# Up-projection of a two-layer decoder trunk: high and low input parts in one 512-column product, the two bank halves added afterwards

## What is computed

```python
h = causal_depthwise_conv(x @ w_ffn_up[i], ffn_conv_w[i], ffn_conv_b[i])   # 2048 -> 2 * 5632, three taps in time
gate, up = jnp.split(h, 2, axis=-1)
ffn = (jax.nn.silu(gate) * up) @ w_ffn_down[i]                              # 5632 -> 2048
ple = (p[i] @ w_ple_proj[i]) * jax.nn.sigmoid(x @ w_ple_gate[i] + b_ple_gate[i])
x = layer_norm(DEEPNORM_ALPHA * x + ffn + ple, ln2_g[i], ln2_b[i])
```

## Time and profile before

| | |
|---|---|
| median of 3 runs | 2536.94 us (2536.22 to 2538.70) |
| span of the profiled execution | 2539.3 us (no other time of this execution is known) |
| TensorE busy in it | 2443.3 us, 96% |
| TensorE weight loads | 2191.4 us, 86% |
| VectorE busy | 1474.3 us, 58% |
| ScalarE busy | 1095.2 us, 43% |
| mean granted TensorE clock | 0.987 |
| layer 1, up-projection loop | 515 to 1022 us |
| layer 2, up-projection loop | 1773 to 2280 us |

### The profile page before, as it was taken

How to read it: one execution, slowest core, us unless ns; L and a number is a source line. 1 busy time by engine, 2 the same in 40 slices (tenths; PEclk the granted TensorE clock), 3 DMA queues, 4 the chain that set the end, 5 groups by cost and what they waited for, 6 DMA issues and landing times.

```text
span 2539.3 us, 38833 instructions
## 1 busy us (share of the span) xinstructions
PE 2443.3 (96%) x15144; PEld 2191.4 (86%) x15144; DVE 1474.3 (58%) x1397; ACT 1095.2 (43%) x1109; POOL 210.8 (8%) x121
## 2 busy tenths in 40 slices
PE   6899999999999999999988999999999999999997
PEld 6777887899999999888777778878999999998885
DVE  4566656475655566544555756564655566565446
ACT  3355435344444444444443554353444444443443
POOL 0144201000000000000011432010000000000000
PEclk9999999999999999999989999999999999999998
DMA  7444555565555555555544444655555555555552
GB/s 230 161 155 146 162 204 184 197 199 182 182 182 182 182 182 182 182 198 189 176 157 161 152 149 149 218 191 190 199 182 182 182 182 182 182 182 184 196 196 102
DMA packets 168228, 455.36 MB, mean 179 GB/s; under 512 B 7545, under 2 KB 11945, under 8 KB 148945
## 3 DMA queue, kind: packets, MB, share of 16 engines
q1 hardware_dynamic: 165536, 440.58, 51.2%
q0 software_dynamic: 2608, 13.69, 1.5%
HBM read 452.14 MB, written 2.10 MB: 179 GB/s over the span
## 4 chain that ended last, share of the span: by engine, by line
PE 85%; issue 7%; DVE 5%; ACT 2%; DMA 1%; POOL 0%; SPq 0%; DVEq 0%; POOLq 0%; ACTq 0%
PE ps L1081 83%; PE ps L1101 1%; ACT w_hi L522 1%; DMA xt<-in_x 0%; DVE w_lo L768 0%; PE ps L1234 0%; DVE xt L822 0%; DVE small L892 0%; DVE xt L818 0%; DVE scratch L895 0%; DMA vec<-in_ln_b 0%; PE ps L1178 0%; PE ps L1205 0%; DVE xT_lo L774 0%; DVE xt L794 0%
## 5 line engine op out<-in xcount | busy, mean ns | idle before, releaser
L768 DVE TENSOR_TENSOR w_lo<-raw,w_hi 128x2048 fp32r<-128x2048 f32 x416 | 969.0, 2330 | 1019.6 <-ACT w_hi L522 1016.7
L522 ACT CAST w_hi<-raw 128x2048 fp32r<-128x2048 f32 x416 | 793.2, 1907 | 1341.9 <-PE ps L1081 1341.9
L1081 PE MATMUL ps<-xT_hi,w_lo 128*128 128x256 f32 x2816 | 797.1, 283 | 1.5 <-DVE work L1025 1.5
L1081 PE MATMUL ps<-xT_lo,w_hi 128*128 128x256 f32 x2816 | 796.9, 283 | 0.0
L1081 PE MATMUL ps<-xT_hi,w_hi 128*128 128x256 f32 x2816 | 796.9, 283 | 0.0
L1081 PE MATMUL ps<-w_lo,xT_hi 128*128 128x512 f32 (+1 forms) x1920 | 753.7, 393 | 34.9 <-DVE w_lo L768 16.5
L1081 PE MATMUL ps<-w_hi,xT_lo 128*128 128x512 f32 (+1 forms) x1920 | 745.2, 388 | 0.0
L1081 PE MATMUL ps<-w_hi,xT_hi 128*128 128x512 f32 (+1 forms) x1920 | 744.9, 388 | 0.0
L1081 PEld LDWEIGHTS ps<-xT_hi,w_lo 128*128 128x128 f32 x2816 | 540.6, 192 | 2.3 <-issue 2.3
L1081 PEld LDWEIGHTS ps<-xT_hi,w_hi 128*128 128x128 f32 x2816 | 540.7, 192 | 0.0
L1081 PEld LDWEIGHTS ps<-xT_lo,w_hi 128*128 128x128 f32 x2816 | 540.7, 192 | 0.0
(11 more groups left out here) (141 smaller groups left out, 1010.1 us busy)
## 6 DMA issues: line engine op xcount, KB each, us to landing
raw<-in_w_ffn_up SPq DMA_DIRECT2D x176, 1024.0 KB, 5.0
raw<-in_w_ffn_down SPq DMA_DIRECT2D x88, 1024.0 KB, 4.8
raw<-in_w_in SPq DMA_DIRECT2D x84, 1024.0 KB, 5.0
raw<-in_w_out SPq DMA_DIRECT2D x32, 1024.0 KB, 5.4
raw<-in_w_ple_gate SPq DMA_DIRECT2D x32, 1024.0 KB, 4.8
vec<-in_ln_g POOLq DMA_DIRECT2D x4, 1024.0 KB, 6.4
vec<-in_ln_b POOLq DMA_DIRECT2D x4, 1024.0 KB, 6.1
raw<-in_w_ple_proj SPq DMA_DIRECT2D x4, 1024.0 KB, 4.8
```

Source lines behind the costliest of these rows:

```text
L522: nc.scalar.copy(w_hi[:, at % SPLIT_SLOTS, :], raw[:, at % RAW_SLOTS, :]).then_inc(hi_split, 1)
L768: tt(w_lo[:, at % SPLIT_SLOTS, :], raw[:, at % RAW_SLOTS, :], w_hi[:, at % SPLIT_SLOTS, :].bitcast(F32), ALU.subtract).then_inc(panels_spl ...
L1081: done = mm(bank, lhs, rhs, start=first and n == 0, stop=last and n == 2, skip_group_check=flip)
```

## The change

`x_hi` and `x_lo` become the two halves of one tile, so that 512 adjacent columns are [x_hi | x_lo] of an input chunk. For each pair (k, c) the two products with w_hi become one matmul of 512 columns into a whole bank, columns 0 to 255 for x_hi and 256 to 511 for x_lo; w_lo by x_hi, 256 columns, is added in the first half of the bank. A half now needs four banks: gate 0 to 3, up 4 to 7. In convolution step 0 ACT copies the second halves of the four banks to SBUF (two instructions of two banks), and DVE adds the first halves to them (two instructions); that sum, `summed`, is what frees the banks, by the new semaphores `gate_summed` and `up_summed`. The convolution reads the sum from SBUF and moves one step back: ACT's four instructions to step 1, DVE's eight to steps 1 and 2, sigmoid and final product to step 3, together with the taps. TensorE waits for the second and fourth `ple_sums` in place of the first and second, and starts the down-projection in the plain order.

```diff
-        xT_hi = sb("xT_hi", [P, KD, SEQ], F32R)
-        xT_lo = sb("xT_lo", [P, KD, SEQ], F32R)
+        xT = sb("xT", [P, KD, 2, SEQ], F32R)
+        xT_hi, xT_lo = xT[:, :, 0, :], xT[:, :, 1, :]
...
+        summed = scratch[:, 0:1024].rearrange("p (c t) -> p c t", t=SEQ)
+        x_lo_part = scratch[:, 1024:2048].rearrange("p (c t) -> p c t", t=SEQ)
...
                 def begin_conv(half, p, i):
-                    if p < 2:
+                    if p == 0:
                         act.wait_ge(panels_used, used(l, UP_AT + 4 * half + 4) + i * UP_BODY)
+                        for c in (0, 2):
+                            nc.scalar.copy(x_lo_part[:, c:c + 2, :],
+                                           ps[:, 4 * half + c:4 * half + c + 2, SEQ:]).then_inc(x_lo_copied, 1)
+                    elif p == 1:
                         act.wait_ge(conv_group_set, layered(l, TAPS, half + 1) + i * 2)
-                        for c in (2 * p, 2 * p + 1):
+                        act.wait_ge((gate_summed, up_summed)[half], layered(l, FF_GROUPS, 2) + i)
+                        stand_alone(act)
+                        for c in range(FF_GROUP):
...
                             last = nc.scalar.activation(
-                                dst, ps[:, 2 * half + p, (c % 2) * SEQ:(c % 2 + 1) * SEQ], ACT.Identity,
+                                dst, summed[:, c, :], ACT.Identity,
                                 bias=conv_group[:, 3, half, c:c + 1], scale=conv_group[:, 2, half, c:c + 1])
-                        last.then_inc(conv_begun, 1)
-                    elif p == 2 and half == 0:
+                            if c % 2:
+                                last.then_inc(conv_begun, 1)
+                    elif p == 3 and half == 0:
...
                 for j in range(4):
                     if j == 0:
                         begin_conv(1, 0, FF_GROUPS - 1)
+                    down_step(j + 1, 0)
+                    if j == 1:
                         begin_conv(1, 1, FF_GROUPS - 1)
-                    down_step(j + 1, 0)
...
-                def convolve(half, p, i):
+                def convolve(half, p, i, taps=True):
-                    if p < 2:
-                        dve.wait_ge(conv_begun, layered(l, 4 * FF_GROUPS, 2 * half + p + 1) + i * 4)
+                    if p == 0:
+                        for c in (0, 2):
+                            dve.wait_ge(x_lo_copied, layered(l, 4 * FF_GROUPS, 2 * half + c // 2 + 1) + i * 4)
+                            stand_alone(dve)
+                            link(tt(summed[:, c:c + 2, :], ps[:, 4 * half + c:4 * half + c + 2, 0:SEQ],
+                                    x_lo_part[:, c:c + 2, :], ALU.add))
+                        dve.sem_inc((gate_summed, up_summed)[half], 1)
+                    elif p < 3:
+                        dve.wait_ge(conv_begun, layered(l, 4 * FF_GROUPS, 2 * half + p) + i * 4)
                         for back in (1, 2):
-                            for c in (2 * p, 2 * p + 1):
-                                u = ps[:, 2 * half + p, (c % 2) * SEQ:(c % 2 + 1) * SEQ - back]
+                            for c in (2 * p - 2, 2 * p - 1):
...
-                        if p == 1:
-                            dve.sem_inc((gate_conv, up_taken)[half], 1)
-                    elif p == 2:
+                        if p == 2 and half == 0:
+                            dve.sem_inc(gate_conv, 1)
+                    else:
+                        if taps:
+                            set_taps(1 - half, i + half)
                         if half == 0:
                             dve.wait_ge(gate_sigmoid, layered(l, FF_GROUPS, 1) + i)
+                            stand_alone(dve)
                         link(tt(group, group, tmp[half], ALU.mult))
-                    else:
-                        set_taps(1 - half, i + half)
...
+            def columns_by_tokens(l, at, i, first_bank, first_chunk, first, last):
+
+                pe.wait_ge(panels_split, layered(l, PANELS, at + 1 + RAW_SLOTS) + i * UP_BODY)
+                s = at % SPLIT_SLOTS
+                for k in range(4):
+                    for c in range(FF_GROUP):
+                        w = slice(k * 512 + c * P, k * 512 + (c + 1) * P)
+                        x = xT[:, first_chunk + k, :, :].rearrange("p s t -> p (s t)")
+                        if first and k == 0:
+                            mm(ps[:, first_bank + c, :], w_hi[:, s, w], x, start=True, stop=False)
+                        done = mm(ps[:, first_bank + c, 0:SEQ], w_lo[:, s, w], xT_hi[:, first_chunk + k, :],
+                                  start=False, stop=False, skip_group_check=True)
+                        if not (first and k == 0):
+                            done = mm(ps[:, first_bank + c, :], w_hi[:, s, w], x, start=False, stop=last and k == 3)
+                done.then_inc(panels_used, 1)
...
-                        pe.wait_ge(ple_sums, layered(l, 4, half + 1))
-                        pe.wait_ge((gate_conv, up_taken)[half], layered(l, FF_GROUPS, 1) + i)
+                        pe.wait_ge(ple_sums, layered(l, 4, 2 * half + 2))
+                        pe.wait_ge((gate_summed, up_summed)[half], layered(l, FF_GROUPS, 1) + i)
+                        stand_alone(pe)
                         for j in range(4):
...
+                            columns_by_tokens(l, UP_AT + 4 * half + j, i, 4 * half, 4 * j, j == 0, j == 3)
...
-                order = [(1, n) for n in range(4)] + [(0, n) for n in range(4)]
-                waits = {(0, 0): (gate_conv, layered(l, FF_GROUPS, FF_GROUPS + 1)),
-                         (0, 2): (up_taken, layered(l, FF_GROUPS, FF_GROUPS + 1))}
+                waits = {(0, 0): (gate_summed, layered(l, FF_GROUPS, FF_GROUPS + 1)),
+                         (1, 0): (up_summed, layered(l, FF_GROUPS, FF_GROUPS + 1))}
```

More of the change, by code:

```diff
@@ L324, in build, with chunks @@
         pool_step = sem("pool_step")
+        def chunks(bank):
+            return ps[:, bank, :].rearrange("p (k t) -> p k t", t=SEQ)
         def rotate(tt, link, heads, table, m, rot_a, rot_b):
@@ L826, in _ @@
             dve.sem_inc(panels_split, RAW_SLOTS)
[L828 to L829 removed]
+            dve.sem_inc(gate_summed, 1)
+            dve.sem_inc(up_summed, 1)
             dve.sem_inc(left_normed, M)
@@ L1053, in _ @@
                         convolve(1, 0, FF_GROUPS - 1)
-                        convolve(1, 1, FF_GROUPS - 1)
                     down_step(j + 1, 0)
-                    if j == 1:
-                        convolve(1, 2, FF_GROUPS - 1)
+                    if j:
+                        convolve(1, j, FF_GROUPS - 1, taps=False)
                 stand_alone(dve)
@@ L1069, in _ @@
             mm = nc.tensor.matmul
+            def columns_by_tokens(l, at, i, first_bank, first_chunk, first, last):
[12 more added lines that the diff above has]
+                done.then_inc(panels_used, 1)
             def panel(l, at, i, step, products, show=False):
                 pe.wait_ge(panels_split, layered(l, PANELS, at + 1 + RAW_SLOTS) + i * step)
-                for at_product, (bank, hi, lo, x_hi, x_lo, first, last, flip, wait) in enumerate(products):
+                for at_product, (bank, hi, lo, x_hi, x_lo, first, last, wait) in enumerate(products):
                     if wait:
@@ L1079, in panel @@
                     for n, (x, w) in enumerate(pairs):
-                        lhs, rhs = (w, x) if flip else (x, w)
-                        done = mm(bank, lhs, rhs, start=first and n == 0, stop=last and n == 2,
-                                  skip_group_check=flip)
+                        done = mm(bank, x, w, start=first and n == 0, stop=last and n == 2)
                     if show and last and at_product < len(products) - 1:
@@ L1096, in tokens_by_columns @@
                         found.append((banks(m, n)[:, 0:hi - lo], w_hi[:, s, lo:hi], w_lo[:, s, lo:hi], xh[x], xl[x],
-                                      first and k == 0, last and k == k_chunks - 1, False, waits.get((m, n))))
+                                      first and k == 0, last and k == k_chunks - 1, waits.get((m, n))))
                 return found
@@ L1367, in down @@
+                def down(j, i, first=False, last=False, waits={}):
                     pe.wait_ge(g_split, layered(l, KFF, j + 1) + i * 4)
-                    wide(l, DOWN_AT + j, j, first, last, i=i, step=4, order=order, waits=waits, show=True)
-                down(0, 0, first=True, order=order, waits=waits)
+                    wide(l, DOWN_AT + j, j, first, last, i=i, step=4, waits=waits, show=True)
+                down(0, 0, first=True, waits=waits)
                 for j in range(1, 4):
```

41 lines of the change are left out of this document (13 added, 28 removed).

## The result

| | before | after |
|---|---|---|
| median | 2536.6 us (4 runs, 2536.22 to 2538.7) | 2519.45 us (4 runs, 2517.09 to 2521.57) |
| ratio of the times | | 0.993 (95% interval 0.9918 to 0.9942) |
| span of the profiled execution | 2539.3 us | 2516.7 us (its time 2518.66) |
| TensorE busy, VectorE, ScalarE | 96%, 58%, 43% | 96%, 61%, 46% |

The change takes 17.2 us off. The forecast was 39.0 us: the direction is right, the gain is less than half, and the time lies 2.5 us above the top of the range, 2517.

What follows compares the result with a forecast made beforehand. TensorE alone was taken to set the pace, each matmul costing its columns plus 13.3 ns. Terms -37.5 + 2.3 - 3.8 = -39.0 us gave 2500.3 against the profiled span, 2497.9 us as median; range 2490 to 2517.

Steps and rivals of the forecast that it cites:

- The products: TensorE's up-projection pairs: three 256-column matmuls become one of 512 and one of 256, 360.0 to 346.7 ns, 37.5 us less.
- the bounds (337 to 360 ns): Limits on a pair's price in the loop, read from the steps where one width follows the other in the earlier trace.
- Rival A: Alternating widths cost extra in the loop: 353 to 357 ns a pair, 2515 to 2527 us, middle 2520; 15%.
- DVE and ACT in the loop: New additions and copies in the up-projection loop are covered by both engines' wait for TensorE: 0 us.
- Semaphore instructions: One added for TensorE at each of 44 half starts: between 0 and 13 us in all, taken as 0.
- rival C: Each of the 44 half starts leaves a gap of 0.1 to 0.3 us: 2502 to 2511 us; 4%.
- Entry: Into the loop, TensorE waits for DVE's second sum, 1.15 us later: 2.3 us more over 2 layers.
- Exit: Out of the loop, the first down-projection panel takes 6.1 us in place of 8.00: 3.8 us less over 2 layers.
- Rival B: Alternating widths cost less in the loop: some 340 ns a pair, gain 56 us, 2479 us; 7%.
- D: Slower: DVE's or ACT's step work passes its window, splits come late, TensorE waits for w_lo; for instance 2555 us; 2%.
- E: The wide product is issued as two, 360 ns a pair; only the transitions' gain is left, 2535 us; 1%.

Runs made afterwards that it cites:

- no break in the alternation: The changed kernel without an opening of its own: each half begins narrow, wide, so widths alternate through all 88 panels of a loop; 2507.3 us, ratio 0.9885.
- groups of 16: The changed kernel with its products reordered: in each panel first all 16 w_lo products of 256 columns, then the 16 wide ones; 2502.94 us, ratio 0.9866.
- the short loads: The changed kernel with wide products, but for those that begin a bank, loading and using only 64 of 128 weight columns; 2485.38 us, one execution.
- the two products of 256: The changed kernel with each wide product issued as two of 256 columns, all else kept; 2536.96 us, ratio 1.0001 to the kernel before.
- the passages halved and the earlier entry: The changed kernel with 16 narrow and 16 wide products grouped, every second panel wide first, and TensorE entering on the first ple sum; 2498.06 us, ratio 0.9846.

## Why the prediction was right or wrong

**The step that failed** is in "The products": "I take 346.7, the sum of the two steady distances: a late and an early step of a like size would cancel in an alternation". The chip can do just that: 117 + 230 = 346.7, 3 early and 3 late, for whole loops (no break in the alternation). But there is a second pattern, 117 + 236.3 = 353.3, where the wide step is 9.6 late and the narrow one 3 early, and in the profiled execution the changed kernel runs in it in 43 of its 44 halves. What makes the two patterns stays open. The term comes to 6.7 ns x 2816 = 18.8 us instead of 37.5. Of the 21.6 us between forecast and median these are 18.7; the stretch at the lower clock behind the entry of layer 2, less the one half in the faster pattern, is 1.1, and the entries and exits together were 0.2 better than forecast (-1.7 for -1.5). The remaining 2.0 is within the spread of the runs.

**What could have been read.** The earlier trace rows had 1021.94, 1022.17, 1022.41, steps of 0.23 and 0.24 us behind a narrow matmul. By the unrounded starts the steps are 234, 236, 228, 232, 231 and then 227 ns, to 1 ns the series that the groups of 16 show behind the narrow ones. In an alternation each wide step is the first of such a row and never settles, so the settled 226.7 was the wrong price for it. The prediction saw the excess, called it a passing state, and did not ask what becomes of a passing state that is set up anew every time. Yet the first steps would not have given the time either: 234, and 113 for the first narrow step behind wide ones (groups of 16), make 347 ns, the faster pattern. Nothing in the rows of before shows the slower one; only the bounds (337 to 360 ns) held it. The lower of these rests on a misread row. In the earlier trace rows the step of 0.11 us was taken for one behind 512 columns, "by way of a stall", but a narrow matmul stands in between:

```profile
1772.80 0.38 PE L1081 MATMUL ps<-xT_hi,w_lo 128*128 128x256 f32 x1 [0.73 <-DVE work L1025]
```

That the first narrow step behind wide ones did come at 113 ns (groups of 16) is luck.

**Rival A** had the price, 353 to 357 ns, and a middle of 2520, and 15%. A panel took 5.65 us, over the 5.62 named as its sign. It is right in the time, not in its reason: there is no fixed extra per change of width, as the same alternation also runs at 346.7. The rule cited beside it, N / 2.4 + 2.5 ns a matmul (the Trainium skill, TensorE: Matmul & The Clock Gate, Back-to-back issue gap, which gives it for an isolated matmul), gave 2528. No run shows it for these products: a pair would take 320 + 5 = 325 ns by it, an estimate, and the fastest measured, with the short loads, took 341.0.

**The range** ended at 2517, 2 us into rival A (2515 to 2527), whose own middle was 2520: so it left out most of A and not the half that the prediction speaks of. That the chance of 15% was too low is a judgement; the trace had an excess that speaks for A, the first steps of 0.23 and 0.24 us, and the steady distance was taken against them.

**The other steps.** DVE and ACT in the loop at 0 us: right, shown by the two products of 256, with both loops at 506.97 us. Semaphore instructions at 0: right, no gap at any half start, so rival C is out. Entry +1.15 each: measured +1.28; what was missed is that a longer wait may be followed by a stretch at the lower clock, 1.5 us in layer 2. Exit -1.9 each: measured -2.13; the cast came 1.16 us behind TensorE's start instead of 1.4, w_lo 1.95 behind it and TensorE 2.76 behind that, as forecast. The banks kept TensorE for a moment (1013.03), which cost nothing, as the panel ends by the same w_lo. Rival B (340 ns) came only with shortened loads, which is not this change. D did not come: TensorE never waits for w_lo inside the loop. E is out: the wide product stands as one matmul of 512 columns in the rows by form.

## What to carry over

The steady distance of a matmul among its like is not its price between others: where a change mixes widths, sum it once from the first distances behind a change of width, and keep the range open to the largest of them (236, with the steady 120 of a narrow matmul, would have been 356 ns a pair here, where 353.3 came). Then try the order: equal widths side by side gave 16.5 us here, with the passages halved and the earlier entry 21.4, where the change itself had given 17.2. And when a wait gets longer at the start of a long stretch of TensorE, look at the granted clock behind it, not only at the wait.

## What the runs showed of the hardware

- The same alternating instructions can run in two patterns, 346.7 and 353.3 ns a pair. The pattern is held for a whole loop of 88 panels where nothing breaks the alternation. It can differ between two loops of one execution and between two executions of one kernel. The two loops of one such execution parted at the second matmul (227 and 235 ns).
- Behind a change from 256 to 512 columns the distances are 233, 236, 228, 233 and 231 ns before they settle at 226.7.
- Wide products with 64 of 128 weight columns bring a pair to 341.0 ns, under both patterns, with the same columns streamed; narrow ones with 64 give 346.9, no less than the faster pattern (one execution each).
- At the lower clock level, 1.2 GHz, the steps are 213 and 427 ns (first panel of layer 2's loop), which is 256 and 512 columns over 1.2 GHz, with none of the 13 ns that the steady steps at 2.4 GHz have.
- Of the 22 entries with 2.4 us from the last start to the first, 7 were followed by 3.4 us at the lower clock (in the changed kernel layer 2 and not layer 1); the four with 1.27 us were not, nor the two of the kernel before with 1.12.
- ACT takes 589 ns for an activation of 256 columns with scale and bias from SBUF, where the same from PSUM took 558 ns before.
